# Norm weights among the constants, input in two halves, squares added by the vector engine, two unscaled blocks of u

## What is computed

```python
h = rms_norm(x, norm_w)                      # y = x * rsqrt(mean(x*x) + EPS), times norm_w
u, z_s, q, k, v, z_a, r_s, r_a = split(h @ w_in)
y_s = s5_branch(u, lam_re, lam_im, log_dt, b, c, d_skip, w_glu)   # a complex diagonal scan over time
y_s = (y_s * silu(z_s)) @ w_ssm_out
q = apply_partial_rope(rms_norm(q, q_norm_w), positions)          # norms per head of 64
k = apply_partial_rope(rms_norm(k, k_norm_w), positions)
y_a = (dilated_attention(q, k, v) * silu(z_a)) @ w_attn_out
x = x + (sigmoid(r_s) * y_s + sigmoid(r_a) * y_a) @ w_o
```

## Time and profile before

| what | us |
|---|---|
| median of 3 runs | 1101.56 |
| the profiled execution, its time | 1103.28 |
| its span, first to last instruction | 1101.5 |
| TensorE busy | 957.5 (87%) |
| VectorE busy | 407.6 (37%) |
| ScalarE busy | 261.6 (24%) |
| GpSimd busy | 157.3 (14%) |
| mean granted clock of TensorE, share of full speed | 0.938 |

### The profile page before, as it was taken

One profiled execution on the slowest core, in us unless ns is written; L12 is line 12 of the kernel. 1 busy time (PEld: TensorE's weight loads), 2 busy tenths in 40 slices (PEclk: granted clock), 3 DMA queues, 4 the chain that ended last, 5 costly groups with the idle time before them and its releaser, 6 DMA issues.

```text
span 1101.5 us, 11971 instructions
## 1 busy us (share of the span) xinstructions
PE 957.5 (87%) x4724; PEld 486.1 (44%) x4724; DVE 407.6 (37%) x701; ACT 261.6 (24%) x637; POOL 157.3 (14%) x107
## 2 busy tenths in 40 slices
PE   8999999999999999999999999976666757677757
PEld 6644444448886448445444454423121313131312
DVE  6789889745521203273523213210110102020201
ACT  3585976424411021311312121000000000000000
POOL 0976687810000000000000000000000000000000
PEclk9999999999999999999999999988787988886987
DMA  9444234442224437544224778999999999999997
GB/s 355 188 152 153 89 141 153 147 144 114 104 89 155 153 140 282 201 152 154 76 77 153 313 323 336 429 426 425 427 428 425 430 428 429 428 425 430 427 428 306
DMA packets 29774, 292.88 MB, mean 266 GB/s; under 512 B 8480, under 2 KB 9376, under 8 KB 10912
## 3 DMA queue, kind: packets, MB, share of 16 engines
q1 hardware_dynamic: 28640, 292.21, 65.5%
q10 hardware_dynamic: 1088, 0.05, 0.1%
HBM read 291.20 MB, written 1.05 MB: 265 GB/s over the span
## 4 chain that ended last, share of the span: by engine, by line
PE 60%; DMA 32%; ACT 3%; DVE 2%; issue 2%; POOL 1%; SPq 0%; DVEq 0%; ACTq 0%; POOLq 0%
DMA mem<-in_experts 32%; PE psum L311 15%; PE psum L316 12%; PE psum L330 8%; PE psum L323 8%; PE psum L1540 3%; PE psum L782 3%; PE psum L1567 1%; PE psum L1868 1%; PE psum L1520 1%; PE psum L1557 1%; PE psum L816 1%; PE psum L876 1%; PE psum L864 1%; PE psum L803 1%
## 5 line engine op out<-in xcount | busy, mean ns | idle before, releaser
L1540 PE MATMUL psum<-mem 128*32 128x512 f32 x1012 | 149.4, 721 | 81.2 <-DMA mem<-in_experts 81.2
L323 PE MATMUL psum<-mem,hT 128*128 128x512 f32 x288 | 126.3, 595 | 0.9 <-ACT mem L621 0.9
L311 PE MATMUL psum<-mem,hT 128*128 128x512 f32 x288 | 125.5, 593 | 0.0
L1540 PEld LDWEIGHTS psum<-mem 128*32 128x32 f32 x1012 | 31.3, 121 | 179.8 <-DMA mem<-in_experts 111.5
L323 PEld LDWEIGHTS psum<-mem,hT 128*128 128x128 f32 x288 | 55.7, 196 | 65.2 <-issue 65.2
L311 PEld LDWEIGHTS psum<-mem,hT 128*128 128x128 f32 x288 | 54.2, 190 | 65.9 <-issue 65.7
L316 PE MATMUL psum<-mem 128*128 128x512 f32 x160 | 69.9, 593 | 0.6 <-ACT mem L1819 0.6
L1685 DVE SCALAR_TENSOR_TENSOR mem<-mem,psum 128x512 f32<-128x512 f32 x8 | 5.5, 689 | 161.7 <-ACT mem L1437 161.7
L316 PE MATMUL psum<-mem,hT 128*128 128x512 f32 x128 | 58.8, 602 | 3.8 <-ACT mem L1819 3.8
L1567 PE MATMUL psum<-mem 128*32 128x512 f32 x256 | 42.1, 793 | 20.6 <-DMA mem<-in_experts 16.5
L330 PE MATMUL psum<-hT,mem 128*128 128x256 f32 x256 | 57.6, 382 | 0.0
(11 more groups left out here) (365 smaller groups left out, 1211.9 us busy)
## 6 DMA issues: line engine op xcount, KB each, us to landing
mem<-in_experts SPq DMA_DIRECT2D x86, 2048.0 KB, 35.7
mem<-in_front SPq DMA_DIRECT2D x39, 2048.0 KB, 7.7
mem<-in_experts SPq DMA_DIRECT2D x18, 1024.0 KB, 33.9
mem<-in_front SPq DMA_DIRECT2D x2, 1024.0 KB, 10.5
xn<-in_xT SPq DMA_DIRECT2D x1, 1024.0 KB, 7.3
mem<-in_ssm_b SPq DMA_DIRECT2D x2, 512.0 KB, 12.7
mem<-in_ssm_c SPq DMA_DIRECT2D x2, 512.0 KB, 18.0
xres<-in_x SPq DMA_DIRECT2D x1, 1024.0 KB, 9.0
```

The lines of the kernel that those rows point to most:

```text
L311: ins = pe.matmul(dst, lhs[:, k, P * i:P * i + P], w[:, k, c0:c0 + 512], start=(k == 0), stop=(k == nk - 1))
L323: ins = pe.matmul(dst, tokens[:, k, i], w[:, k, :], start=(k == 0), stop=(k == KD - 1))
L1540: ins = pe.matmul(banks[m // 2 % 2][32 * q:32 * q + 32, :], xgT[:, k, 32 * q:32 * q + 32], w[q][:, FF * kk:FF * kk + FF], start=(k == 0), ...
```

## The change

Four things are changed, all at the start of the first layer.

The norm weights of q and k that three of ScalarE's small loads brought are laid out beforehand in the second part of the constants, 102 more columns of it. The wait of line 1016 is now for the positions alone, and that of line 649 for the second part of the constants.

The input comes in two loads of half the features each, and the first half of u's first unit in two loads of one block each. Squares and gains wait for their half, blocks 0 and 1 of u for their own load.

The squares are added by VectorE, three additions over 512 columns after the eight gains, so that TensorE sums them in two matmuls instead of eight. This sum stands behind block 0 of u. There are five of the first matmuls instead of six.

Blocks 0 and 1 of u both work on the unscaled input. VectorE scales block 0 ahead of the eight chunks, and block 1 behind them, where ScalarE copied block 1 before.

```diff
-        qkw = small[:, 148:244].rearrange("p (c n) -> p c n", c=6)
+        qkw = C("qk_rows").rearrange("p (c n) -> p c n", c=6)
-        qk_col = small[:, 694:700]
+        qk_col = C("qk_columns")
...
         def sync_of_first_layer(sp):
             sp.dma_start(con[:, 0:NCONST1], A["constants"][:, 0:NCONST1]).then_inc(con_in, 16)
-            sp.dma_start(x_turned, A["xT"]).then_inc(xT_in, 16)
-            sp.dma_start(ring[:, 0, 0:2048], A["front"][0, :, 0:2048]).then_inc(u_half, 16)
+            for n in range(2):
+                sp.dma_start(x_turned[:, 4 * n:4 * n + 4, :], A["xT"][:, 4 * n:4 * n + 4, :]).then_inc(xT_in[n], 16)
+            for n in range(2):
+                sp.dma_start(ring[:, 0, 1024 * n:1024 * n + 1024], A["front"][0, :, 1024 * n:1024 * n + 1024]).then_inc(u_block_in[n], 16)
             sp.dma_start(ring[:, 0, 2048:4096], A["front"][0, :, 2048:4096]).then_inc(slot_loaded[0], 16)
...
         def scalar_of_first_layer(act):
 
-            for c, name in enumerate(("q_norm_w", "k_norm_w")):
-                act.dma_start(qkw[:, 3 * c:3 * c + 3, :], A[name][0, :, 0:16].partition_broadcast(P)).then_inc(misc_in, 16)
-            act.dma_start(qk_col, A["qk_columns"]).then_inc(misc_in, 16)
             act.dma_start(posi[:, :], A["att_positions"]).then_inc(misc_in, 16)
...
-            act.wait_ge(xT_in, 16)
             for n in range(4):
+                act.wait_ge(xT_in[n // 2], 16)
...
-            for j in range(1, 4):
+            for j in range(2, 4):
                 take_u(j)
...
             act.wait_ge(c_scaled, 1)
-            act.wait_ge(misc_in, 64)
+            act.wait_ge(con2_in, 16)
...
-            for n in range(6):
+            for n in range(5):
                 pe.matmul(banks[7][:, 0:256], ident, con[:, 0:256], start=True, stop=True)
-            for k in range(KD):
-                pe.wait_ge(sq_done, k // 2 + 1)
-                ins = pe.matmul(tp.tile(TP_X)[:, 0:256], C("ones"), squares[:, 256 * k:256 * k + 256], start=(k == 0), stop=(k == KD - 1))
-            tp.filled(ins, TP_X)
+
+            def sum_of_squares():
+                pe.wait_ge(sq_added, 3)
+                for k in range(2):
+                    ins = pe.matmul(tp.tile(TP_X)[:, 0:256], C("ones"), squares[:, 256 * k:256 * k + 256], start=(k == 0), stop=(k == 1))
+                tp.filled(ins, TP_X)
...
-                    elif s == 1:
+                    elif s == 2:
                         pe.wait_ge(hT_ready, k + 1)
...
-            for m in range(4):
+            project_u(0, 0)
+            sum_of_squares()
+            for m in range(1, 4):
                 project_u(0, m)
...
             def gains_onto_input():
-                dve.wait_ge(xT_in, 16)
                 for k in range(KD):
+                    dve.wait_ge(xT_in[k // 4], 16)
                     dve.tensor_scalar(raw[:, k, :], x_turned[:, k, :], normw[:, k:k + 1], None, ALU.mult).then_inc(raw_ready, 1)
+
+                for n in range(2):
+                    dve.wait_ge(sq_done, 2 * n + 2)
+                    a, b = (squares[:, 512 * m:512 * m + 512] for m in (2 * n, 2 * n + 1))
+                    dve.tensor_tensor(a, a, b, ALU.add).then_inc(sq_added, 1)
+                dve.wait_ge(sq_added, 2)
+                dve.tensor_tensor(squares[:, 0:512], squares[:, 0:512], squares[:, 1024:1536], ALU.add).then_inc(sq_added, 1)
...
+                scale_u(0)
                 for k in range(KD):
                     dve.tensor_tensor(hT[:, k, :], raw[:, k, :], rows1, ALU.mult).then_inc(hT_ready, 1)
-                pj.to_read(dve, PJ_U)
-                pj.emptied(dve.tensor_tensor(uT[:, 0, :], pj.tile(PJ_U)[:, 0:256], rows1, ALU.mult), PJ_U)
+                scale_u(1)
...
-                dve.wait_ge(misc_in, 64)
+                dve.wait_ge(misc_in, 16)
```

More of the change, by code:

```diff
@@ L35 @@
                 ("none", 128), ("causal", 128), ("mask0", 512), ("mask1", 512), ("tri64", 64), ("slots", 32), ("upper", 128),
-                ("chunk0", 256), ("cos2", 64), ("sin2", 64), ("rev4", 4), ("rev8", 8),
+                ("chunk0", 256), ("cos2", 64), ("sin2", 64), ("rev4", 4), ("rev8", 8), ("qk_rows", 96), ("qk_columns", 6),
                 ]
@@ L189, in qk_columns, with qk_rows @@
     return np.concatenate([gains, gains], 1).T
+def qk_rows(inputs):
+    gains = np.concatenate([inputs["q_norm_w"][0], inputs["k_norm_w"][0]])[:, :16]
+    return np.broadcast_to(gains.reshape(1, 96), (P, 96))
 def column_layout(inputs):
     return np.concatenate([inputs[name][0].reshape(KD, P).T for name in ("norm_w", "d_skip")], 1)
-LAID_OUT = ("positions", "lam_re", "lam_im", "log_dt", "b_re", "b_im", "c_re", "c_im", "norm_w", "d_skip", "norm_mix_2")
+LAID_OUT = ("positions", "q_norm_w", "k_norm_w", "lam_re", "lam_im", "log_dt", "b_re", "b_im", "c_re", "c_im", "norm_w", "d_skip", "norm_mix_2")
 FRONT = ([(f"u{n}", "w_in", W1COLS["u"] + 512 * n, 8) for n in range(2)]
@@ L261, in build @@
         con = sb("con", [P, NCONST])
-        small = sb("small", [P, 1024])
+        small = sb("small", [P, 972])
         psum = stack.enter_context(nc.psum_tensor("psum", [P, 8, 512], F32))
@@ L431, in build @@
         ropcos = small[:, 582:598].rearrange("p (i n) -> p i n", i=2)
-        hss = [small[:, 972 + 16 * n:988 + 16 * n] for n in range(3)]
+        hss = [small[:, 148 + 16 * n:164 + 16 * n] for n in range(3)]
         hrs = [small[:, 646 + 16 * n:662 + 16 * n] for n in range(3)]
@@ L466, in build @@
             last_fill[name] = s
-        con_in, con2_in, u_half, xT_in, misc_in, bt_in, ct_in, xre_in = (sem(s) for s in (
-            "con_in", "con2_in", "u_half", "xT_in", "misc_in", "bt_in", "ct_in", "xre_in"))
+        con_in, con2_in, misc_in, bt_in, ct_in, xre_in = (sem(s) for s in (
+            "con_in", "con2_in", "misc_in", "bt_in", "ct_in", "xre_in"))
+        u_block_in = [sem(f"u_block{n}_in") for n in range(2)]
+        xT_in = [sem(f"xT_in{n}") for n in range(2)]
+        sq_added = sem("sq_added")
         act1, dve1, pool1 = Signal(sem("act_step1")), Signal(sem("dve_step1")), Signal(sem("pool_step1"))
@@ L779, in project_u @@
                         pe.wait_ge(raw_ready, k + 1)
-                    elif s == 1:
+                    elif s == 2:
                         pe.wait_ge(hT_ready, k + 1)
-                    ins = pe.matmul(pj.tile(s)[:, 0:256], w[:, m, k, :], (hT if s else raw)[:, k, :], start=(k == 0), stop=(k == KD - 1))
+                    ins = pe.matmul(pj.tile(s)[:, 0:256], w[:, m, k, :], (raw if s < 2 else hT)[:, k, :], start=(k == 0), stop=(k == KD - 1))
                 pj.filled(ins, s)
@@ L2237 @@
     par = ssm_layout(source)[0]
-    for name, a in (("columns", column_layout(source)), ("ssm_par", par), ("norm_mix", source["norm_mix_2"][0].reshape(KD, P).T)):
+    for name, a in (("qk_rows", qk_rows(source)), ("qk_columns", qk_columns(source)), ("columns", column_layout(source)), ("ssm_par", par), ("norm_mix", source["norm_mix_2"][0].reshape(KD, P).T)):
         at, width = CONST_AT[name]
```

6 lines of the change are left out of this document (4 added, 2 removed).

## The result

The changed kernel has a median of 1105.72 us (1103.31 to 1106.93, 13 runs) against 1101.56 (1099.99 to 1102.9, 13 runs): a ratio of 1.0033, interval 1.0025 to 1.0040, slower by 2.8 to 4.4 us. The ratio puts it at 1105.2, at the upper end of the range on record; the median itself is 0.4 us above that range. The profiled execution took 1106.54 us, 3.3 more than the one of before; its span is 1104.7 (1101.5 before).

What follows compares the result with a forecast made beforehand. The prediction took TensorE to bound the first part and expert weights the last, with two nearly level branches starting the dense run. From the median 1101.56, -0.4 (VectorE's branch) and +1.7 (clock) gave 1102.9 us, range 1100.4 to 1105.3.

Steps and rivals of the forecast that it cites:

- the first of its two terms: VectorE's branch up to c_scaled: the dense run starts at 42.25 instead of 42.64, counted as -0.4 us.
- C: Rival at the loads: they come no earlier, u's first block lands at 9.8, result 1104.9 us; chance 0.13.
- part 2: TensorE until the rows are scaled: block 0 of u starts at 7.8, the sum of squares ends at 12.15.
- part 3: VectorE until the parameters, then GpSimd's 15.15 us as before: c_scaled at 42.05, TensorE waiting 4.85 us, a 0.4 us gain.
- the overlap as moved and not changed: GpSimd's products: the scans and angle sum beside them stay the same and only come earlier, so 15.15 us carries over.
- B: Rival at GpSimd's products: VectorE beside them slows them, c_scaled 3.4 us later, 1106.3 us in all; chance 0.12.
- part 4: TensorE after its wait for c_scaled: low clock for about 3.4 us of dense work, losing 1.7 us (bounds 0 and 3.4).
- its last test: Prediction wrong if the time from L323's start to the end isn't the old one plus the clock's share.
- A: Rival at the wait before the dense run: the clock stays up, result 1101.2 us; chance 0.13.
- D: Rival at GpSimd's branch: it shortens too, the dense run starts 3.8 us earlier, 1097.8 us; chance 0.09, other gains included.
- E: Rival at the loads: each half pays its own fixed time, result 3.4 us later than forecast, 1106.3 us; chance 0.03.
- "same": Outcome for the whole kernel: neither below 1099.4 us (faster) nor above 1103.8 us (slower); chance 0.58.

Runs made afterwards that it cites:

- hold_vector: The changed kernel with one further wait: VectorE begins its first pair of state groups only when c_scaled is raised; 1106.49 us.
- decay_first: The changed kernel with VectorE's 15 decay_factors instructions moved directly behind the scaling of the rows, in front of the angle tables; 1107.60 us.
- fill_wait: The changed kernel with twelve unused matmuls in TensorE's wait for c_scaled; 1102.44 us; its mark (a TensorE group near 300 us) at 300.82, against 304.04.
- whole_loads: The changed kernel with x in one load and the first half of u's first unit in one load again; 1105.33 us.
- sum_first: The changed kernel with the two matmuls that sum the squares ahead of block 0 of u instead of behind it; 1107.00 us.
- one_unscaled: The changed kernel with one unscaled block of u instead of two, block 1 working on the scaled input again; 1103.12 us.
- gap_one_unscaled: The rope_in_gap kernel with one unscaled block of u instead of two; 1104.57 us.
- rope_in_gap: The changed kernel with the rope's angles and four coarse angle table instructions moved into VectorE's wait before the reciprocal; 1098.30 us.
- before_decay_first: The kernel before the change, with VectorE's decay_factors moved ahead as in decay_first; 1103.94 us.
- gap_no_copy: The rope_in_gap kernel without GpSimd's small copy that raises c_scaled; 1099.28 us.
- before_weights: The kernel before the change, with only the norm weights of q and k put among the constants; 1100.08 us.

## Why the prediction was right, and where it was off

The direction of the sum was right (+1.3 on record, 2.8 to 4.4 measured), and so was its mechanism: TensorE's head start buys nothing, it ends in front of c_scaled, and the longer idle time brings the low clock. The size wasn't, and the first of its two terms had the wrong sign: the start of the dense run moved by +1.91 us and not by -0.4. So the direction hung on the clock's term alone. That the ratio lies just inside the range is in part luck, too: its upper end was set by C, loads that come no earlier, and C didn't happen. The tail of VectorE's work was met almost exactly: from the sum's end to the last scaled block 5.76 us (5.79 foretold), from there to the parameters 8.81 as before. Three terms were mis-sized, all in one direction.

- **The start of block 0 and the sum's end** (part 2: 7.8 and 12.15; measured 8.57 and 13.5). Of this, 0.8 us is the loads: I let them run at 409 GB/s from the constants on, and they passed at 346 GB/s between 3.7 and 8.5 us. Another 0.4 to 0.5 us is the clock at the start: TensorE's first 16 passes on u took 3.9 us instead of 3.45. So VectorE's branch became 0.95 us longer and not 0.4 shorter. The landing was within the bound I had set (9.8), but the value taken was near the wrong end.
- **GpSimd's products and COPY** (part 3: 15.15 us carried over; measured 16.11). The step failed that took the overlap as moved and not changed. Half of the 0.96 us is in the six products, 15.05 us from the first one's start to the last one's end (43.28) against 14.56: the scans of the first pair and the angle sum behind them now slow three products (3.34, 2.71 and 2.35, against 2.37, 1.91 and 1.91 with VectorE held in hold_vector), where they slowed two (2.83 and 3.15, against 1.91 and 2.34). The other half is the COPY itself, 1.00 us instead of 0.53: u came early, so VectorE was at the scans of its second pair (42.59) by then. I had B as a rival at 3.4 us; it is 0.96 in this kernel, and VectorE's whole effect on the branch is 3.1 (hold_vector). The Trainium skill, "GPSIMD Engine Reference", section Specifications, says that GpSimd shares its SBUF interfaces with VectorE and that VectorE instructions with two SBUF inputs contend there. The traces agree: beside GpSimd a rotation with an input in PSUM takes 0.69 us, as it does alone, and a pair of scans takes 4.45, against 2.33 with GpSimd idle (at 42.41 in decay_first).
- **The clock** (part 4: 1.7; measured 2.8, by the stretches and by fill_wait's mark). The low stretch behind the wait was 5.7 us long and not 3.4; I had given twice the stretch as a bound. After the same idle time in whole_loads it was 3.7 us.

Three readings of the prediction are off without moving the sum. The row of GB/s from 3 us on isn't nearly empty: it has 143 to 145 in three slices and a mean near 78, low beside 409, so the argument stands. The gain of TensorE at its head was 4.4 us by the prediction's own numbers (u done at 37.4, before at 41.78) and not 5.2; 2.8 was measured. And by its last test, that the time from the dense run's start to the end be the old one plus the clock's share, the profiled executions fall short: 1060.2 against 1058.9 us is 1.3 more, not 2.8. Up to the mark the test holds (259.49 against 256.67, 2.8 more); the missing 1.5 us lie behind it, where executions differ by up to 3.4.

A was wrong, C and D didn't happen, and of E there is at most a fifth of its price (some 0.6 of 3.4 us, by the estimate above). By the median the result is on the slower side of the 1103.8 that the prediction set, to which it gave 0.33. The chances were too kind to "same" (0.58): each of the three terms had its bound on the side of slower, and I added up their middles.

## What to carry to other kernels

Before making a branch faster, find the wait at which it meets another, and read from the trace how far apart the two are. Here the other was already 0.2 us the later, so the 2.8 us by which u was done earlier had nothing to buy, and what lengthened the other branch by 1.9 went straight to the end. An idle time of TensorE of several microseconds in front of dense work is to be priced at its length plus the low clock behind it (1.4 to 2.8 us here), and filling it with unused matmuls is a cheap test of that price. And small work of VectorE was cheapest where GpSimd is idle: the variant that put it beside GpSimd's products was 1.9 us slower than the change, the one that moved it out of VectorE's tail into a wait 7.4 faster.

## What the runs showed of the hardware

- Beside a running GpSimd instruction over 128x1024, a VectorE instruction over 32 elements in SBUF took 1.8 us instead of 0.19: L1114 and L1115 of decay_first ended within 0.05 us of the GpSimd instruction beside each. A TENSOR_SCALAR over 512 elements took 2.46 instead of 0.43. Those that began just before a GpSimd instruction kept their time: L1113 at 22.47 took 0.18 (GpSimd began at 22.50), L1116 at 26.36 took 0.69 (GpSimd began at 26.37, and its product took 2.90 instead of 2.37). That the order of starting decides isn't isolated by a run.
- Within the first 120 us of these kernels idle times of TensorE of 2.53 and 3.84 us (hold_vector), 2.74 and 3.10 (sum_first), 3.23 (one_unscaled), 3.30 (gap_one_unscaled), 5.57 (whole_loads), 5.58 (the change) and 7.53 (decay_first) were each followed by the low clock. Those of 1.84 us (rope_in_gap), 1.85 (before_decay_first) and 1.26 (gap_no_copy) weren't. The low clock covered 2.8 to 5.7 us of the work behind it.
- Three small loads on ScalarE's queue, two of them of 24 KB in pieces of 64 bytes, kept 1 MB on SyncE's queue 1.9 us from being complete (8.5 with them, 6.6 without, before_weights).
